# Three RMS norms of a two-block transformer kernel: sums of squares taken tile by tile on TensorE

## The reference

```python
def rms_norm_2(x, g):
    y = x * lax.rsqrt(jnp.mean(x * x, axis=-1, keepdims=True) + RMS_EPS)
    return y * g

for layer in range(2):
    if layer == 1:                       # keys and values of MLA
        hn_kv = rms_norm_2(h, kv_in_g)   # -> w_dkv, w_kr
    hn = rms_norm_2(h, mix_pre_g[layer])
    m = conformer_conv(hn, ...) if layer == 0 else mla_attention(hn, ...)
    h = h + rms_norm_2(m, mix_post_g[layer])
    f = squared_relu_mlp(rms_norm_2(h, ffn_pre_g[layer]), w_ff1[layer], w_ff2[layer])
    h = h + rms_norm_2(f, ffn_post_g[layer])
```

## Time and profile before

| what | value |
|---|---|
| median of 3 runs | 1921.63 us (1921.1 to 1922.07) |
| span of the profiled execution | 1917.8 us |
| runs' median above that span | 3.8 us; the profiled execution's own time is taken as span + 3.8 |
| TensorE busy | 1813.4 us, 95% |
| VectorE busy | 992.4 us, 52% |
| ScalarE busy | 628.4 us, 33% |
| GpSimd busy | 257.3 us, 13% |
| GpSimd adds of squares (line 476) | 61 of 1449 ns |
| chain that ended last | PE 74%, DVE 16%, ACT 5%, issue 4% |

### The profile page before, as it was taken

The page is one execution under the profiler, slowest core; times in us unless marked ns, Lnnn a source line. Parts: engine busy times, 40 slices in busy tenths (PEclk is TensorE's granted clock), DMA queues, the critical chain, the costliest instruction groups (busy, mean ns, idle before and its releaser), DMA issues.

```text
span 1917.8 us, 21982 instructions
## 1 busy us (share of the span) xinstructions
PE 1813.4 (95%) x8052; PEld 1462.6 (76%) x8052; DVE 992.4 (52%) x1290; ACT 628.4 (33%) x923; POOL 257.3 (13%) x216
## 2 busy tenths in 40 slices
PE   6999999999999999978999999988998999999996
PEld 5777978878888787857888788867666878878885
DVE  4575246663664399946542343365644374324433
ACT  4334134432343333434321222243323243112220
POOL 2100011110111122313210011120000131001111
PEclk9998799999999999968999999999889999999998
DMA  4212023332232222302332222312200213222221
GB/s 176 78 55 67 1 88 107 98 120 89 87 98 94 72 92 84 110 22 78 99 99 92 94 89 97 99 44 88 88 0 1 77 57 108 99 90 96 92 84 44
DMA packets 43841, 156.01 MB, mean 81 GB/s; under 512 B 4864, under 2 KB 4992, under 8 KB 43776
## 3 DMA queue, kind: packets, MB, share of 16 engines
q1 hardware_dynamic: 43632, 154.19, 24.5%
q10 hardware_dynamic: 144, 0.92, 0.1%
HBM read 153.00 MB, written 2.10 MB: 81 GB/s over the span
## 4 chain that ended last, share of the span: by engine, by line
PE 74%; DVE 16%; ACT 5%; issue 4%; POOL 0%; ACTq 0%; DVEq 0%; DMA 0%; POOLq 0%; SPq 0%
PE bank L991 22%; PE bank L992 21%; PE bank L993 21%; DVE cv L1832 4%; DVE w_lo L1527 3%; DVE a_lo L1545 1%; PE bank L1475 1%; ACT w_hi L600 1%; ACT w_hi L590 1%; DVE h L1901 1%; DVE m L1894 1%; DVE tmp L1758 1%; PE bank L1059 1%; PE bank L1143 1%; PE bank L1478 1%
## 5 line engine op out<-in xcount | busy, mean ns | idle before, releaser
L991 PE MATMUL bank<-a_hi,w_hi 128*128 128x512 f32 x1252 | 503.3, 402 | 49.9 <-DVE w_lo L1527 19.7
L1527 DVE TENSOR_TENSOR w_lo<-w_raw,w_hi 128x1024 fp32r<-128x1024 f32 x283 | 367.6, 1300 | 317.8 <-ACT w_hi L590 192.7
L992 PE MATMUL bank<-a_lo,w_hi 128*128 128x512 f32 x1252 | 498.7, 398 | 0.0
L993 PE MATMUL bank<-a_hi,w_lo 128*128 128x512 f32 x1252 | 496.5, 397 | 0.0
L991 PEld LDWEIGHTS bank<-a_hi,w_hi 128*128 128x128 f32 x1252 | 239.5, 191 | 116.6 <-issue 20.4
L993 PEld LDWEIGHTS bank<-a_hi,w_lo 128*128 128x128 f32 x1252 | 239.7, 191 | 52.7
L992 PEld LDWEIGHTS bank<-a_lo,w_hi 128*128 128x128 f32 x1252 | 240.0, 192 | 50.9 <-issue 0.5
L991 PE MATMUL bank<-g_hi,w_hi 128*128 128x512 f32 x688 | 269.6, 392 | 4.7 <-DVE tmp L1924 3.3
L993 PE MATMUL bank<-g_hi,w_lo 128*128 128x512 f32 x688 | 269.9, 392 | 0.0
L992 PE MATMUL bank<-g_lo,w_hi 128*128 128x512 f32 x688 | 269.1, 391 | 0.0
L590 ACT ACTIVATE w_hi<-w_raw 128x1024 fp32r<-128x1024 f32 x167 | 173.7, 1049 | 161.4 <-PE bank L993 161.3
(11 more groups left out here) (272 smaller groups left out, 1900.8 us busy)
## 6 DMA issues: line engine op xcount, KB each, us to landing
w_raw<-in_stream SPq DMA_DIRECT2D x283, 512.0 KB, 3.4
h<-in_xT SPq DMA_DIRECT2D x8, 256.0 KB, 7.0
out<-h SPq DMA_DIRECT2D x8, 256.0 KB, 2.0
cst_b<-in_consts SPq DMA_DIRECT2D x1, 896.0 KB, 9.5
cst_b<-in_consts ACTq DMA_DIRECT2D x1, 896.0 KB, 4.5
cols<-in_vectors SPq DMA_DIRECT2D x1, 289.0 KB, 2.8
cst<-in_consts SPq DMA_DIRECT2D x1, 257.0 KB, 8.4
w_al<-in_w_alpha SPq DMA_DIRECT2D x1, 128.0 KB, 10.0
```

The source lines that it names most:

```text
L991: pe.matmul(out, w0, x0, start=start, stop=False, skip_group_check=loose)
L992: pe.matmul(out, w0, x1, start=False, stop=False, skip_group_check=loose)
L993: return pe.matmul(out, w1, x0, start=False, stop=stop, skip_group_check=loose)
L1527: dve.tensor_tensor(w_lo[slot][:, :], w_raw[slot][:, :], f(w_hi[slot][:, :]), ALU.subtract)\
```

## The change

For the three norms named in `PE_SUMS`, GpSimd no longer adds squares. The square of every tile k goes into one of three buffers in turn (`pe_sq_buf`), and TensorE sums it over the partitions by itself (`tile_sum`), with four one-column products that accumulate in bank 5 over all eight tiles. `three_tiles` issues the sum of tile k - 1 behind the products of tile k, and the sum of the last tile at the end, ahead of the spread. ScalarE waits before the square of tile k for the sum of tile k - 3, whose buffer it takes (`square_for_pe`). `take_root` reads bank 5. The spread, which overwrites bank 4, waits in addition until `post_norm` has added all its tiles.

```diff
+PE_SUMS = ("ffpre0", "pre1", "ffpre1")
...
-    _s, _a = _s + _n, _a + (max(_n - 2, 0) if _name != "ln_var" else KD // 2)
+    _s += _n
+    if _name not in PE_SUMS:
+        _a += max(_n - 2, 0) if _name != "ln_var" else KD // 2
...
+        sq_summed = sem("sq_summed")
...
+        def pe_sq_buf(k):
+            return ssum[:, :] if k % 3 == 0 else sq_buf[k % 3 - 1]
...
-            add_squares("ffpre0")
...
-                    add_squares("pre1")
...
-                    add_squares("ffpre1")
...
+            def square_for_pe(name, k, src):
+                if k == 0:
+                    act.wait_ge(stat_done, STAT_NO[name])
+                if k >= 3:
+                    act.wait_ge(sq_summed, (KD - 1) * PE_SUMS.index(name) + k - 2)
+                act.activation(pe_sq_buf(k), src, ACT.Square, scale=float(D) ** -0.5).then_inc(sq_ready, 1)
...
-                    square(stat, k, T(h, k))
+                    square_for_pe(stat, k, T(h, k))
...
-                take_root(stat, r_pre)
+                take_root(stat, r_pre, sums=5)
...
-                square("pre1", k, T(h, k))
+                square_for_pe("pre1", k, T(h, k))
...
-            take_root("pre1", r_pre)
+            take_root("pre1", r_pre, sums=5)
...
+            def tile_sum(name, k):
+                pe.wait_ge(sq_ready, SQ0[name] + k + 1)
+                for b in range(NB):
+                    last = pe.matmul(bank[5][:, b:b + 1], T(pe_sq_buf(k), b, P), cst[:, ONES:ONES + 1],
+                                     start=(k == 0 and b == 0), stop=(k == KD - 1 and b == NB - 1),
+                                     skip_group_check=True)
+                last.then_inc(sq_summed if k < KD - 1 else stat_done, 1)
+
             def spread(name):
 
                 pe.wait_ge(r_tok_ready, STAT_NO[name] + 1)
+                before = STATS[STAT_NO[name] - 1][0]
+                if name in PE_SUMS and before in H0:
+                    pe.wait_ge(h_ready, H0[before] + KD)
...
-                            if j == 0 and stat_name:
+                            if j == 0 and stat_name and stat_name not in PE_SUMS:
                                 stat(stat_name)
+                    if k and stat_name in PE_SUMS:
+                        tile_sum(stat_name, k - 1)
+                if stat_name in PE_SUMS:
+                    tile_sum(stat_name, KD - 1)
```

## The result

The median went from 1921.63 to 1935.87 us (nine runs of each), which is a quotient of 1.0074; the recorded comparison of the runs gives a ratio of 1.0084 with a 95% interval of 1.0062 to 1.0106: slower, as predicted. The forecast was 1934, which is a ratio of 1.0064.

The account below looks back on a forecast made before the run. TensorE, busy 95% of the span, was taken as the bound. Added sets outweigh closed holes: +4.53 us each in A and C, +3.12 in B, together +12.2; 1921.6 becomes 1933.8, say 1934 us, range 1929 to 1940.

Parts of the forecast that it names:

- Who sets the pace: Inside the three norm stretches: TensorE bounds; GpSimd slows VectorE by 0.67 us a tile; TensorE's holes total 5.9 us.
- B: Stretch of the second norm (pre1), first product on the new operand to unit dq 0; 22.40 us, forecast 25.52.
- C: Stretch of the third norm (ffpre1), first product on the new operand to the next product's tile 3; 23.20 us, forecast 27.73.
- The price of an isolated set: Four one-column products with their loads between dense products: 0.90 to 0.98 us of TensorE's time, 0.94 taken.
- The end that lost its cover: End of A and C, ahead of the spread: root and reciprocal no longer beside six products, a wait of 0.73 us.
- Slow products: First products of each stretch, at 0.43 instead of 0.23 us; 12, 8 and 12 taken, uncertain by about 0.8 us a stretch.
- New waits: In the stretches, square k waits for set k - 3, with a_hi and a_lo behind: slack 4.0 us, cost 0.
- 1 (sets hidden beside dense work): In the stretches, sets run beside dense products: 1911.8 us at zero price; chance 0.04 clearly faster, 0.04 nothing measured.
- 2 (a fall at the end of A or C): Granted clock falls there, about 2.4 us each: one fall 1936.2 us, both 1938.6; chance 0.27 of at least one.
- A: Stretch of the first norm (ffpre0), first product on the new operand to the next product's tile 3; 23.20 us, forecast 27.73.
- 3 (a low clock inside): Clock stays or falls low inside a stretch, a third being one-column work: 12 us a stretch, 1946 to 1970; chance 0.06.
- 4 (sets at 1.2 us): Sets cost more between dense products than at their end, say 1.2 us: +4.7 us, 1938.5; chance 0.07.

Follow-up runs that it names:

- e1_no_adds: From the kernel before, GpSimd's adds left out of the three norms with nothing in their place; 1918.14 us against 1921.23, ratio 0.9981.
- e2_one_set: The changed kernel with only the last tile's set kept; stretches 61.37 us against 80.85, one execution 1919.6 us.
- e5_double: The changed kernel with every set issued twice, the second into an unread bank; stretches 36.43, 33.97 and 36.41 us, 26.0 above the changed kernel.
- e3_both: The changed kernel with GpSimd's adds put back on a spare buffer nobody reads; stretches 26.87, 25.30 and 26.91 us, 1.77 shorter together.
- e4_cover: The changed kernel with set 6 ahead of the last tile's products and set 7 behind its first three; 1942.44 us against 1913.88, ratio 1.0149.
- the wide form: The changed kernel with one 512-column product, ones as weight, replacing each set, and no spread; 1921.20 us against 1913.88 before, ratio 1.0028.
- e13_before_third: The kernel before, unchanged, profiled a third time; 147.1 us at the lower clock level outside the stretches.
- e7_before_again: The kernel before, unchanged, profiled a second time; stretches within 68.71 to 68.80 us, eight slow products behind the middle norm's stall.

## Why the prediction was right, point by point

- *Who sets the pace.* Right. Without GpSimd's adds TensorE is busy in the whole window and the holes are 5.0 us (`e1_no_adds`) of the 5.9 forecast; the difference is two slow products more in B and two in C than the working assumed, and VectorE's pace had hidden these counts (68.71 to 68.80 whatever they are).
- *The price of an isolated set*, the number without a row. 0.90 to 0.91, the low end of 0.90 to 0.98; 0.94 was taken. The six sets between products cost 5.4 us a stretch instead of 5.64. Taking sets out gives 0.90 at equal counts of slow products, doubling them 0.90. The reason that the prediction gives, a weight load with every product, was argued: no run tells the load's share from that of the fp32 form.
- *The end that lost its cover.* Right: 0.71 us of wait against 0.73; the spread behind a wait takes 0.91 instead of 0.81.
- *Slow products.* The counts of before were carried over (12, 8, 12), and came as 12, 12, 9. This made B 0.8 us longer and C 0.5 shorter; with the cheaper sets B was 0.6 over its forecast of 25.5 and C 0.6 under its 27.7. That the sum, 12.05 against 12.2, is nearer than its parts is luck: these two errors cancel.
- *New waits, B's spread, `w_hi`, the spread's added wait.* Right at 0; the waits are in the rows of VectorE and ScalarE above. The stall behind B's spread did move whole, 2.89 us; that the products behind it would run slow, 1.6 to 1.8 us, was not in the sum.
- *The step from span to median.* The span came at 1934.2 and not 1930.0. In every profiled run of the study whose own time is known, that time lies 1.8 us above its span, so the first profile of before was an execution of about 1919.6, by luck 2 us under its median, and a span forecast from it came out 2 us low. The forecast of the median doesn't hang on that, for it comes to 1921.6 + 12.2. Outside the stretches the forecast had 0; the span has 4.35 more there, 3.3 of them by the rate of low time above, and the fall behind B's stall is in it. Both medians are above the forecast, by 1.9 and 1.5 us, which is about what that fall costs and also well inside what the rest of the span does by itself.
- *Rivals.* 1 (sets hidden beside dense work) is refuted by `e2_one_set` and `e5_double`. 2 (a fall at the end of A or C) didn't happen in three profiles of after, but did in `e3_both` and `e5_double`, so some of the runs behind the median may have it; it cost 1.6 us there in `e3_both`, not 2.4. 3 (a low clock inside) didn't happen where nine products stand between two sets, doubled or not, and did in A and B of `e4_cover`, where three do. 4 (sets at 1.2 us) is refuted.

## What to carry to other kernels

Relieving an engine pays only as far as it sets the pace: here the holes that VectorE left were 5 us, and what was put into TensorE's queue to close them cost 17. Price a small product by a row that shows what it costs, not by its columns: four fp32 products of one column cost as much as four of 512 columns in the rounded form, and the sum over partitions with the ones as weight does the same work in one of these. Whatever shortens a stretch has to be followed to the next wait behind it: the wide form lost its 7 us, mostly to one reciprocal, and got them back, in part, when that stood behind the work that TensorE needed next.

## What the runs showed of the hardware

- VectorE's reciprocal of 128x512 in fp32 takes 3.35 us, where its other operations on the same tile take 0.69 to 0.75, and the reciprocal of the four columns 0.18.
- In `e4_cover` TensorE's clock fell to 1.2 GHz with TensorE never idle, at the end of A and of B, behind three sets with three 512-column products among them; behind the same work in C of the same run it stayed at 2.4 GHz.
- A set of four fp32 products of one column took 0.90 us of TensorE's time between dense products, in `e2_one_set`, `e5_double` and the changed kernel alike.
- The same 83 products of the attention stage took 30.0 us at a granted clock of 0.56 in one execution and 24.1 us at 0.77 in another, with TensorE busy 29.5 and 22.9 of them.
- Outside the stretches the kernel before took 6.1 us longer in one execution than in another, with 15.8 us more at the lower clock level (`e13_before_third`, `e7_before_again`).
- A VectorE operation slowed by GpSimd goes from 0.74 to 1.53 us and costs nothing where TensorE is the bound (`e3_both`).
